# HGRN scan of a hybrid backbone step: ScalarE takes the next chunk's turned keys and decay one unit later

## What is computed

```python
def hgrn_scan(q, k, v, log_f, s0):
    ...
    def step(S, inp):
        qc, kc, vc, lf = inp
        b = jnp.cumsum(lf, axis=2)
        dec = masked_exp(tri, b[:, :, :, None, :] - b[:, :, None, :, :])
        A = jnp.einsum('bhik,bhjk,bhijk->bhij', qc, kc, dec)
        o = jnp.einsum('bhik,bhkv->bhiv', qc * jnp.exp(b), S) + A @ vc
        bl = b[:, :, -1]
        S = S * jnp.exp(bl)[..., None] + jnp.einsum('bhck,bhcv->bhkv', kc * jnp.exp(bl[:, :, None] - b), vc)
        return S, o
```

## Time and profile before

| | |
|---|---|
| time, median of 3 | 2480.26 us (2475.42 to 2483.65) |
| the profiled execution's own time | 2479.59 us |
| its span, first to last instruction | 2477.8 us |
| TensorE busy, matmuls | 2155.5 us, 87% |
| VectorE busy | 1463.5 us, 59% |
| ScalarE busy | 1262.7 us, 51% |
| GpSimd busy | 743.7 us, 30% |
| mean granted TensorE clock, share of full | 0.914 |

### The profile page before, as it was taken

How to read it: one execution, slowest core, us unless ns; L and a number is a source line. 1 busy time by engine, 2 the same in 40 slices (tenths; PEclk the granted TensorE clock), 3 DMA queues, 4 the chain that set the end, 5 groups by cost and what they waited for, 6 DMA issues and landing times.

```text
span 2477.8 us, 60210 instructions
## 1 busy us (share of the span) xinstructions
PE 2155.5 (87%) x25872; PEld 1339.7 (54%) x25872; DVE 1463.5 (59%) x1859; ACT 1262.7 (51%) x1674; POOL 743.7 (30%) x570
## 2 busy tenths in 40 slices
PE   5998996878989999999899768788949999999990
PEld 4765656655565555555766557654534444444440
DVE  3255735559362121125476755386369999999976
ACT  2443742346534243333443743265258777887852
POOL 0432113432314242433231233333122333332321
PEclk8999987879999999999999877698969999999995
DMA  9322980020212221316230000020266677990023
GB/s 273 99 84 87 307 273 6 5 55 4 71 52 87 66 102 51 102 51 174 85 106 3 1 5 4 3 56 22 98 250 199 235 254 276 333 317 35 26 102 135
DMA packets 214974, 278.61 MB, mean 112 GB/s; under 512 B 28129, under 2 KB 188493, under 8 KB 214607
## 3 DMA queue, kind: packets, MB, share of 16 engines
q1 hardware_dynamic: 203776, 243.60, 30.3%
q0 software_dynamic: 8576, 30.41, 3.3%
q10 hardware_dynamic: 2383, 1.11, 0.2%
HBM read 368.15 MB, written 29.11 MB: 160 GB/s over the span
## 4 chain that ended last, share of the span: by engine, by line
PE 53%; issue 16%; DVE 14%; POOL 7%; ACT 6%; DMA 2%; SPq 1%; POOLq 0%; DVEq 0%; ACTq 0%
PE ps L2246 50%; POOL mix L952 5%; DVE arena L1629 3%; DMA wbuf<-in_w_mod 1%; DVE mix L1629 1%; DVE mix L1637 1%; ACT arena L1127 1%; PE ps L2453 1%; DVE xT L1629 1%; DVE hT L1629 1%; DVE mix L1633 1%; DVE yg L1629 1%; POOL mix L955 1%; DVE arena L1633 1%; SPq L687 1%
## 5 line engine op out<-in xcount | busy, mean ns | idle before, releaser
L2246 PE MATMUL ps<-hT,mix 128*128 128x512 f16 (+2 forms) x3024 | 378.9, 288 | 24.8 <-DVE hT L1629 15.1
L2246 PE MATMUL ps<-w,xgT 128*128 128x512 f16 x1632 | 366.0, 381 | 1.2 <-ACT xgT L1514 1.2
L2147 DVE SCALAR_TENSOR_TENSOR w<-wst,w 128x2048 f16<-128x2048 f32 x136 | 309.8, 2319 | 24.4 <-ACT w L1500 24.3
L2246 PEld LDWEIGHTS ps<-hT,mix 128*128 128x128 f16 x3024 | 229.8, 99 | 172.6 <-issue 18.7
L985 POOL TENSOR_TENSOR a<-aval,a 128x256 f16<-128x256 f32 x68 | 158.6, 2332 | 378.8 <-ACT a L1543 378.8
L2246 PEld LDWEIGHTS ps<-w,xgT 128*128 128x128 f16 x1632 | 157.6, 98 | 180.3 <-issue 3.7
L1500 ACT ACTIVATE w<-wst 128x2048 f16<-128x2048 f32 x136 | 251.4, 1899 | 0.0
L2246 PE MATMUL ps<-mix 128*128 128x512 f16 (+5 forms) x1856 | 210.7, 297 | 15.1 <-POOL mix L955 8.8
L2246 PE MATMUL ps<-hT,arena 128*128 128x128 f16 (+1 forms) x1440 | 198.5, 299 | 0.7 <-DVE const L1629 0.7
L2246 PE MATMUL ps<-w2m,aT 128*128 128x512 f16 x816 | 188.9, 381 | 2.6 <-DVE aT L2179 2.6
L2246 PEld LDWEIGHTS ps<-mix 128*128 128x128 f16 (+3 forms) x1856 | 126.5, 132 | 90.0 <-POOL mix L955 12.4
(11 more groups left out here) (360 smaller groups left out, 3577.0 us busy)
## 6 DMA issues: line engine op xcount, KB each, us to landing
wst<-in_moe_w SPq DMA_DIRECT2D x204, 1024.0 KB
wbuf<-in_w_mod SPq DMA_DIRECT2D x40, 1024.0 KB
wbuf<-in_ffn_w SPq DMA_DIRECT2D x33, 1024.0 KB
wbuf<-in_w_in SPq DMA_DIRECT2D x20, 1024.0 KB
xs_rows<-in_table SPq DMA_DIRECT2D x17, 512.0 KB, 6.4
xg<-xs_rows POOLq DMA_DIRECT2D x17, 512.0 KB, 5.2
ys_rows<-yb POOLq DMA_DIRECT2D x17, 512.0 KB, 4.2
wbuf<-in_w_out SPq DMA_DIRECT2D x32, 256.0 KB
```

What stands on the lines that cost most here:

```text
L2147: v_.scalar_tensor_tensor(out=q[1], in0=staged(s, p), scalar=WS, in1=q[0], op0=ALU.mult, op1=ALU.subtract).then_inc(sg["m_lo13"], 1)
L2246: return mm_(o, w, x, start=first, stop=last, skip_group_check=True)
```

## The change

ScalarE's two instructions of `keys(n + 1)` are issued in the second unit of chunk n instead of the first: they come behind `wide(4n)` and behind `decays(4n + 3)`.

```diff
--- before.py
+++ after.py
@@ -1360,7 +1360,7 @@
                         decays(u + 2)
                     if x == 0 and n:
                         place(n - 1)
-                    if x == 0 and n < 4:
+                    if x == 1 and n < 4:
                         keys(n + 1)
                     wide(u)
                     if x == 2 and n < 3:
```

## The result

The changed kernel takes 2514.89 us (median of 4, 2510.19 to 2518.34) against 2477.84 us for the kernel before (median of 4, 2473.53 to 2483.65): a ratio of 1.0127, with a 95% interval of 1.010 to 1.0154. It is slower. In a later comparison on one chip it was 2514.83 against 2484.50 us, 1.0126 (1.010 to 1.0151). The two medians of the changed kernel agree, those of the kernel before differ by 6.7 us, so the loss is 30 to 37 us. The forecast was 2500 us (20.7 us of loss) with a range of 2488 to 2508: the direction was right, the size too small by a third to a half.

A forecast was written before the change was run, and what follows sets the result against it. The HGRN loop was taken as a ring of three engines with little slack, no engine alone the bound. 2479.6 us plus 12.7 of waits and 8.0 of low clock made 2500.3, stated as 2500 us, range 2488 to 2508.

The forecast's parts named there:

- K behind D: Sign on ScalarE: the two moved instructions, L1005 and L1276, stand behind the decays, L1290 and L1291.
- gaps before P(6), P(10), P(14): Sign on VectorE: gaps before its masked products of units 6, 10 and 14, which empty the attention matmuls' results.
- The waits: HGRN loop, three carries per layer waiting for slot 1 (bank pair 1): 11.8 us lost at VectorE's products.
- Chunk 0: Slot 1 goes to the norm's sums (rs0): wait of 0 in layer 0; 0.9 us plus 1.0 us clock in layer 1.
- The clock term: TensorE at its lower clock behind the new gaps: 7.0 us for six carries plus 1.0 us at rs0, 8.0 us.
- the values of E and A: Clock price taken from TensorE's exponents' (E) and attention (A) matmuls behind old gaps: 1.5 us per long gap, 1.0 per short.
- The upper end of the range: 2508 us, with all carries at the low clock.
- (a): Rival: the waits come but the clock does not fall, or falls where TensorE would idle anyway; 2492 us, 22%.
- (b): Rival: VectorE is the real bound and its slack hides the carry's lateness; 2481 to 2485 us, 8%.
- (c): Rival: faster, as the moved instructions leave the front of ScalarE's unit at eight places; 2470 us, 3%.
- (d): Rival: worse, the low clock holds through every carry, 2508 us, or a new issue stall in layer 0; 7%.
- The stalls and the slow last carry: TensorE late in layer 1's loop: at most 3.9 us could come back if these went away; taken as 0.

The follow-up runs named there:

- chunk0: Changed kernel with only chunk 1's keys moved, those of chunks 2 to 4 left in place: 2486.98 against 2484.50 us for the kernel before, ratio 1.0009.
- behind_wide: Changed kernel with the moved keys issued behind the wide copies but ahead of the decays, in the first unit: 2498.99 against 2484.50 us for the kernel before.
- the late pair: TensorE's carry and VectorE's update one unit later, in the changed kernel and in the kernel before: 2493.60 and 2494.95 us against 2482.25 for the kernel before.
- the second trace of before: The kernel before run once more without any edit, for a second trace: 2484.6 us.
- filler_gap: Changed kernel with extra overwritten matmuls in the gap ahead of the carry, chunks 1 to 3: 2489.21 against 2482.25 us for the kernel before, ratio 1.0028.
- filler: Changed kernel with 12 or 5 extra overwritten matmuls ahead of the attention matmuls that precede the carry: 2506.60 against 2484.50 us for the kernel before.

## Why the prediction was wrong in size

**The place and the mechanism were right.** Rows, releaser and order came as written: K behind D, each carry 0.1 us behind the end of L1276, gaps before P(6), P(10), P(14), clock 0.50 in the carry. chunk0, behind_wide and the late pair show that it is the wait of the carry for slot 1 that costs.

**The waits were right in size.** Predicted losses: 1.55, 2.2, 2.35 us and 1.5, 1.9, 2.3 us. Measured, as 10.06 less the step of before: 1.69, 2.26, 2.50 and 1.70, 2.05, 2.49 us, together 12.7 against 11.8 (the second trace of before gives the same 12.7). Of the 0.9 us, 0.6 is a slip in adding: the terms that the prediction lists from the end of P(4n) (3.16 us of instructions, five gaps of 0.04, two hand-overs of 0.08) make 3.5 us and not 3.4, and 3.51 is what the carries show.

**Chunk 0 was right**, -0.3 and +2.3 us from E(2) to P(4) against 0 and 1.9 with its clock part; rs0 did go on at the low level.

**The clock term failed.** It said 7.0 us for the six carries, with the step "I take the values of E and A, since the low stretch ended within or soon after them". Measured, as the changed kernel's step less 10.06: 2.9, 2.8, 1.5 us in layer 0 and 3.1, 3.1, 1.4 us in layer 1, 14.8 us in the first trace and 13.7 us in the second. Two errors lie in that step. The price was taken from matmuls that lose little: E(10) and A(8) went from 2.45 to 3.63 us, a half more, while the carry at the low clock goes from 3.41 to 5.84 us, and the rows for exactly that stood in the earlier trace rows. And the low stretch goes on past the carry into E (1.51 and 1.89 us instead of 1.04), which was in no bound: I had capped the price at the carry's 2.4 us. The carries themselves lost 11.0 us of the 14.8, and E and A behind them 3.8. The 12.7 + 14.8 us, and 1.9 us for chunk 0, less 0.2 us of scatter in the rest, make the 29.2 us that the two loops grew by. The forecast had 20.7: the clock of the six carries is 7.8 us of the difference, the waits 0.9.

**The upper end of the range** was the carries at the low clock, 2508 us. It left out the E's share and the variation from one execution to the next, which alone is up to 9 us ahead of the loop. With the price from the carry's own rows (6 x 2.4 us) the forecast would have been that same 2508 us, 28 us of loss, near the 29.2 us of the loops. That would have been partly luck: only two of the six carries ran at the low clock throughout, and what the others kept is about what E and A lost.

**Rivals.** (a), the clock does not fall or does not matter, is refuted by filler_gap. (b), hidden, and (c), faster, fell by the result. (d), at 7%, is nearest to what happened: in the first trace the low clock held through C(0) of each layer (mean granted clock 0.50) and through more than half of the time of the other four (0.56 to 0.71). The stalls and the slow last carry of layer 1's last stretch did not go away (22.3, 22.5 and 22.9 us), as taken; but the second trace of the kernel before has 19.8 us there, so that stretch varies without any edit.

**The skill's rules.** The Trainium skill, "TensorE: Matmul & The Clock Gate", Part 1, puts the penalty of the ramp at under 1% of a typical span and advises against fitting a count of slow matmuls. It says this of the warm-up; that the clock would be left out of a comparison is the forecast's reading of it and goes further than the page. Here the low clock of the six carries was worth 14.8 us, 0.6% of the span, and yet more than the waits. The Trainium skill, "Runtime: NRT & Kernel Launch", Instruction fetch mechanics, calls the cost of fetching the next block of instructions mostly hidden. In layer 0 of the kernel before TensorE stood on "issue" for 4.17 us; no run shows that this was a fetch, so it neither bears out nor refutes the page. The changed kernel did not show that stall ahead of A(2) at all, but a wait of 2.24 us for L1276 at rs0, and chunk 0 ended 0.3 us earlier.

## What to carry to other kernels

Before moving a read of a buffer later, find the next writer of that buffer and what stands behind it in its engine's order: the data may not be wanted for three units, while the slot is wanted at once. When a move makes TensorE wait, price the stretch behind the wait at the low clock with rows of just those matmuls and of what follows them, and carry the case that the clock falls with a chance of its own even for a short gap: it fell here behind 1.27 us. To tell a wait from its clock, fill the gap with matmuls whose result is overwritten, and compare the steps around the gap and not the time, since the fill changed a distant stretch too (5.3 us here).

## What I had not expected of the hardware

The clock fell behind gaps of 1.27 and 1.35 us, and it stayed full behind one of 2.44 us ([2.44 <-ACT extra L1276] above, carry 3.41 us). In one trace (filler, layer 0) two gaps of 1.35 us were followed by a carry of 5.07 and one of 3.40 us. In the same program the same carry ran at either level in two executions (3.41 and 4.54 us). The length of the gap alone did not tell which. Gaps of 0.19 to 0.27 us left the clock at the full level in all six places.
